# SBUF tensors allocated in another order: TensorE's split operands and the arena start at multiples of 1024 bytes

## The reference

```
for i in range(2):                                   # first block
    x = x + (attention if i == 0 else pooling)(rms_norm(x, norm_mix[i]))
    h = relu(rms_norm(x, norm_mlp[i]) @ w_up[i])     # 1024 x 4096
    x = x + (h * h) @ w_down[i]                      # 4096 x 1024
x = rms_norm(x, norm_final)
u = rms_norm(x) @ w_in                               # second block, 1024 x 7840
x = x + merge(gates, ssd(u) @ w_ssd_out, latent(u) @ w_mla_out) @ w_o
x = x + cross_attention(rms_norm(x), memory)         # w_xq, w_xkv, w_xo
y = sum over 2 of 32 experts: (silu(h @ w_gate[e]) * (h @ w_up[e])) @ w_down[e]
out = rms_norm(x + y)
```

## Time and profile before

| | before |
|---|---|
| median of 3 runs | 1366.15 us (1365.02 to 1366.16) |
| span of the profiled execution, first to last instruction | 1363.2 us |
| TensorE matmul busy | 1309.7 us, 9405 matmuls |
| VectorE busy | 1032.2 us |
| ScalarE busy | 872.8 us |
| DMA | 279.78 MB, mean 205 GB/s |
| mean granted TensorE clock | 0.992 |

### The profile page before, as it was taken

One profiled execution on the slowest core, in us unless ns is written; L12 is line 12 of the kernel. 1 busy time (PEld: TensorE's weight loads), 2 busy tenths in 40 slices (PEclk: granted clock), 3 DMA queues, 4 the chain that ended last, 5 costly groups with the idle time before them and its releaser, 6 DMA issues.

```text
span 1363.2 us, 23818 instructions
## 1 busy us (share of the span) xinstructions
PE 1309.7 (96%) x9405; PEld 1202.4 (88%) x9405; DVE 1032.2 (76%) x1535; ACT 872.8 (64%) x1289; POOL 78.2 (6%) x81
## 2 busy tenths in 40 slices
PE   7999999999999999999999899999998999999994
PEld 7989999998999998999999888999986777777773
DVE  6776655568555568998998886874569999999994
ACT  6565444546444546675656766654457999999994
POOL 0001000001000000000001100110000111011113
PEclk9999999999999999999999999999999999999997
DMA  8644555553655544555435534454436999999963
GB/s 276 205 152 130 191 185 185 185 186 94 202 185 187 187 140 145 178 161 158 150 102 181 193 122 155 155 186 161 157 156 254 365 360 354 351 366 365 362 261 123
DMA packets 150108, 279.78 MB, mean 205 GB/s; under 512 B 13721, under 2 KB 122238, under 8 KB 136574
## 3 DMA queue, kind: packets, MB, share of 16 engines
q1 hardware_dynamic: 141952, 269.97, 57.0%
q0 software_dynamic: 7696, 8.41, 2.0%
q10 hardware_dynamic: 366, 0.12, 0.0%
HBM read 274.26 MB, written 21.50 MB: 217 GB/s over the span
## 4 chain that ended last, share of the span: by engine, by line
PE 75%; DVE 15%; ACT 5%; issue 3%; DMA 1%; ACTq 0%; DVEq 0%; POOLq 0%; POOL 0%; SPq 0%
PE psum L852 18%; PE psum L854 18%; PE psum L853 18%; DVE weights_parts L2692 3%; PE psum L1413 3%; PE psum L1412 3%; PE psum L1411 3%; DVE weights_parts L2086 2%; PE psum L1437 2%; DVE arena L2476 2%; PE psum L1439 2%; PE psum L1438 2%; ACT weights_parts L1933 1%; ACT weights_parts L1476 1%; PE psum L1256 1%
## 5 line engine op out<-in xcount | busy, mean ns | idle before, releaser
L2086 DVE TENSOR_TENSOR weights_parts<-ring,weights_parts 128x1024 fp32r<-128x1024 f32 (+3 forms) x312 | 363.4, 1184 | 161.5 <-ACT weights_parts L1476 161.1
L1476 ACT ACTIVATE weights_parts<-ring 128x1024 fp32r<-128x1024 f32 (+3 forms) x312 | 309.0, 1010 | 175.6 <-PE psum L854 174.8
L852 PE MATMUL psum<-xnorm_parts,weights_parts 128*128 128x256 f32 x884 | 255.5, 289 | 6.0 <-DVE xnorm_parts L2235 2.0
L853 PE MATMUL psum<-xnorm_parts,weights_parts 128*128 128x256 f32 x884 | 249.0, 282 | 0.0
L854 PE MATMUL psum<-xnorm_parts,weights_parts 128*128 128x256 f32 x884 | 248.9, 282 | 0.0
L852 PE MATMUL psum<-expert_cols,weights_parts 128*128 128x256 f32 (+1 forms) x688 | 194.7, 283 | 3.3 <-DVE expert_cols L2104 2.0
L854 PE MATMUL psum<-expert_cols,weights_parts 128*128 128x256 f32 (+1 forms) x688 | 192.1, 279 | 0.0
L853 PE MATMUL psum<-expert_cols,weights_parts 128*128 128x256 f32 (+1 forms) x688 | 191.9, 279 | 0.0
L852 PE MATMUL psum<-hidden_parts,weights_parts 128*128 128x256 f32 x640 | 181.9, 284 | 2.6 <-DVE hidden_parts L2544 1.7
L853 PE MATMUL psum<-hidden_parts,weights_parts 128*128 128x256 f32 x640 | 180.5, 282 | 0.0
L854 PE MATMUL psum<-hidden_parts,weights_parts 128*128 128x256 f32 x640 | 180.5, 282 | 0.0
(11 more groups left out here) (422 smaller groups left out, 2528.3 us busy)
## 6 DMA issues: line engine op xcount, KB each, us to landing
expert_raw<-in_w_exp_down SPq DMA_DIRECT2D x35, 1024.0 KB, 7.6
ring<-in_mlp_w_up SPq DMA_DIRECT2D x32, 1024.0 KB, 5.4
ring<-in_mlp_w_down SPq DMA_DIRECT2D x32, 1024.0 KB, 4.9
ring<-in_w_in SPq DMA_DIRECT2D x30, 1024.0 KB, 5.3
ring<-in_w_exp_gate SPq DMA_DIRECT2D x23, 1024.0 KB, 5.0
ring<-in_w_exp_up SPq DMA_DIRECT2D x23, 1024.0 KB, 7.3
ring<-in_attn_w_qkv SPq DMA_DIRECT2D x12, 1024.0 KB, 8.4
expert_raw<-in_w_exp_gate SPq DMA_DIRECT2D x12, 1024.0 KB, 5.0
```

The lines of the kernel that those rows point to most:

```text
L852: pe.matmul(out, lh, rh, start=start, stop=False, **more)
L853: pe.matmul(out, lh, rl, start=False, stop=False, **more)
L1476: ins = act.activation(high, src, ACT.Copy)
L2086: ins = dve.tensor_tensor(low, src, high.bitcast(F32), ALU.subtract)
```

## The change

It reorders the calls of `sb`, and nothing else. Five small tensors come first (896 bytes together), then `weights_parts`, `xnorm_parts`, `hidden_parts`, the arena and its parts, then all the rest. No size, instruction or semaphore changes, and each engine has the same instructions in the same order (7240 rows on TensorE, 1100 on DVE, 958 on ACT, 28 on POOL, 246 on SP, all equal).

```diff
+        dtn = sb("dtn", [P, 5, SH])
+        dskip_all = sb("dskip_all", [P, SH])
+        dskip = sb("dskip", [P, ZT])
+        gain_both = sb("gain_both", [P, KT])
+        place_ids = sb("place_ids", [P, 8], I32)
+        w_parts = sb("weights_parts", [P, 2 * UNITS * UNIT], F32R)
+        x_parts = sb("xnorm_parts", [P, 2 * KT * TOK], F32R)
+        hid_parts = sb("hidden_parts", [P, 4 * 512], F32R)
+        with nc.sbuf_tensor("arena", [P, ARENA], F32) as arena:
+            pass
+        moe_units = sb("expert_parts", [P, M_RAW - M_UNITS], F32R)
+        moe_raw = sb("expert_raw", [P, M_COLS - M_RAW])
+        with nc.sbuf_tensor("expert_cols", [P, M_END - M_COLS], F32R) as moe_cols:
+            pass
+        results = sb("results", [P, M_END - M_COLS])
+        arena_rest = sb("arena_rest", [P, ARENA - M_END])
         ring = sb("ring", [P, SLOTS, SLOT])
         consts = sb("consts_sb", [P, C_N])
-        w_parts = sb("weights_parts", [P, 2 * UNITS * UNIT], F32R)
         cols = sb("cols", [P, 2 * P])
-        dskip = sb("dskip", [P, ZT])
-        dskip_all = sb("dskip_all", [P, SH])
...
-        x_parts = sb("xnorm_parts", [P, 2 * KT * TOK], F32R)
-        hid_parts = sb("hidden_parts", [P, 4 * 512], F32R)
...
-        with nc.sbuf_tensor("arena", [P, ARENA], F32) as arena:
-            pass
-        moe_units = sb("expert_parts", [P, M_RAW - M_UNITS], F32R)
...
-        arena_rest = sb("arena_rest", [P, ARENA - M_END])
         psum = ctx.enter_context(nc.psum_tensor("psum", [P, 8, 512], F32))
```

More of the change, by code:

```diff
@@ L364, in build_two_blocks @@
         std_col = sb("std_col", [P, 2, TB])
-        gain_both = sb("gain_both", [P, KT])
         smax = sb("smax", [P, 3, 2])
@@ L374, in build_two_blocks @@
         unit_pair = sb("unit_pair", [2 * SH, SH], F32R)
-        dtn = sb("dtn", [P, 5, SH])
         router_w = sb("router_w", [P, KT, EG + NE])
@@ L379, in build_two_blocks @@
         eps_col = sb("eps_col", [P, 3])
-        place_ids = sb("place_ids", [P, 8], I32)
         slot_rows = sb("slot_rows", [P, NB], I32)
```

## The result

| | before | after |
|---|---|---|
| median | 1366.16 us (4 runs, 1365.02 to 1366.27) | 1374.84 us (4 runs, 1374.51 to 1375.06) |
| ratio, with its 95% interval | 1 | 1.0065 (1.0051 to 1.0079) |
| span of the profiled execution | 1363.2 us | 1373.0 us |

The change costs 0.65%, 8.7 us. The forecast, 1348.0 us, had the wrong sign. The time lies inside the wide range of 1320 to 1386 us, in its slower part, because that range was stretched towards the slower rival. It lies outside the forecast's own 1335 to 1362 us. The rival that happened is "both streams in step", at a smaller price than it was given.

A forecast was written before the change was run, and what follows sets the result against it. TensorE, in flight 96% of the span, was taken as the bound, with DVE at 96% in the experts. 16.0 + 2.1 = 18.1 us off 1366.15 gave 1348.0 us; own range 1335 to 1362, 8 in 10: 1320 to 1386.

The forecast's parts named there:

- the wide range of 1320 to 1386 us: Whole kernel: range for 8 in 10, reaching to half of the much faster and half of the slower case.
- both streams in step: Every split matmul: equal left-overs make the reads collide, up to 122.5 and 245 ns, 1387 to 1408 us; chance 0.27.
- Matmuls of 256 columns: Split matmuls with tokens, expert_cols or weights moving: 21.8 us less TensorE time, of which 16.0 us reaches the end.
- Between them I take 115.0 ns: New distance of 256-column split matmuls, chosen between bounds of 107.5 and 122.5 ns.
- Two operands at the same left-over have shown 113.3: Reason given for 115.0 ns: weights moving, expert_cols stationary, both at 32 mod 64, ran at 113.3 ns.
- The shares passed on: Part of TensorE's 256-column gain reaching the end: 0.5 in 500 to 900 us (DVE at 85%), 0.9 elsewhere.
- Matmuls of 512 columns: Experts, 1260 matmuls: 233.3 to 230.0 ns, 4.2 us, half counted as DVE is at 96%: 2.1 us off.
- the straddled piece: Operand fetch in 64-byte pieces: 512-column moving weights 32 bytes off cover 33 pieces for 2048 bytes, fewer once aligned.
- DVE and ACT: Low parts take 1220 ns from ring and expert_raw alike, so no effect of place: cost 0.
- Transfers: Gate pieces land 5.0 us after issue; aligned destinations might save about 3% of a transfer, hidden by DVE: cost 0.
- The places don't matter: Rival for all streams: distances stay among the known ones, nothing happens, 1364 to 1368 us; chance 0.18.
- The count in 50 to 500 us: Quickest test in the profile after: TensorE matmuls in that stretch, 3693 before, about 3% more at 115.0 ns.

The follow-up runs named there:

- the half-low one of the change: Changed kernel with DVE writing only half of the low parts of the experts' weights from the 7th unit on: 1358.35 us, 0.9947.
- the second and fourth experiment: Changed kernel with 32 bytes ahead of xnorm_parts: 1360.48 us; changed kernel with weights_parts and xnorm_parts at 32, hidden_parts 64, arena 96: 1363.68 us.
- the half-low pair: Kernel before and changed kernel, each with DVE writing half of the experts' low weight parts from the 7th unit on: 1353.04 and 1358.35 us.
- the run at 80, 112 and 240: Changed kernel, weights 16 bytes later and padding, start differences 80 (xnorm_parts), 112 (hidden_parts), 240 (expert_cols): 1370.17 us, one run.

## Why the prediction was wrong, point by point

**The step that failed** is the one under "Matmuls of 256 columns": "Between them I take 115.0 ns". It was chosen from the left-over mod 64 of each operand by itself. What sets the distance of these tensors, all at multiples of 32, is the difference of the two starts mod 256. None of the pairs read in the earlier trace rows has the difference 0; they have 224, 64, 192 and 32. "Two operands at the same left-over have shown 113.3" took 32 and 32 mod 64 for the same place, but mod 256 that pair stands 192 apart. The rows could not give the number for 0, and the interpolation was read as if they could.

**The terms of the sum.** 118.3 to 120.0 ns costs 4572 x 1.7 = 7.8 us, 117.8 to 120.0 costs 2064 x 2.2 = 4.5, 116.7 to 120.0 costs 288 x 3.3 = 1.0. Another 192 matmuls, with the weights moving and expert_cols stationary, had no term in the prediction: 114.5 (three quarters at 113.3, one at 118) to 120.0, 1.1 us. Sum 14.4 us against the 21.8 off that was forecast. At the experts' start 12.3 of it have arrived, 0.85. The shares passed on had been put at 0.9, and at 0.5 in the stretch with DVE at 85%, and the half was about right. The weight loads that began at 500, 900 and 1000 us before begin 8.0, 10.5 and 12.3 us later. So 500 to 900 us adds 2.5 us, where the mean distances give 4.5 (2170 matmuls with xnorm_parts or hidden_parts moving, 400 with expert_cols, 48 with the weights), 0.56. The two other traces with these distances, the half-low one of the change and the old order with 32 bytes, show 2.5 us there as well. 50 to 500 us adds 8.0, 6.3 and 7.7 us in the three traces, where the distances give 6.9. So the share did not fail; the sign and the size of the distance did.

**Matmuls of 512 columns.** The sign was right, the size somewhat too small and the reason wrong: 226.7 ns with weights_parts moving against xnorm_parts, 229.2 with expert_parts moving and 229.8 in the down product, not 230.0, and the second and fourth experiment refute the straddled piece. 420 x 6.6 + 420 x 4.1 + 420 x 3.3 = 5.9 us of TensorE's time, of which 2.5 arrive, 0.4 and not quite "half". With DVE relieved, 5.5 arrive. That DVE caps it was right, and the half-low pair shows it.

**DVE and ACT** at no cost: right. The groups by form of the kernel after, which answer to the earlier trace rows:

```profile
L2692 DVE TENSOR_TENSOR expert_parts<-ring,expert_parts 128x1024 fp32r<-128x1024 f32 x46 | 55.2, 1218 | 0.0
...
L2692 DVE TENSOR_TENSOR expert_parts<-expert_raw,expert_parts 128x1024 fp32r<-128x1024 f32 x24 | 28.9, 1219 | 0.0
```

**Transfers** at no cost: right in the sum. By the Trainium skill, "DMA: Bandwidth & Descriptors", section "How a descriptor splits into AXI transactions", a row of 8192 bytes takes 32 transactions for 33 once its destination is aligned, as an estimate 3% less time. The landing times show no such gain, 5.4 and 5.2 us for 5.0, and the median packet of 8192 bytes takes 309 ns in both kernels. But the alignment does show in single packets, in the direction of the rule. Of the packets of 1024 bytes between 50 and 1000 us, 5.6 to 5.9% take longer than 46 ns, their median, in the three kernels whose ring starts at a multiple of 256 (the change, its half-low version, and the run at 80, 112 and 240), and 13.9 to 18.1% in the other eleven. That is worth little, mean 52.1 ns for 52.4, and no time here hangs on it.

**The rivals.** "The places don't matter" is out: 1.0065 against 1.0003 for the old left-overs in the new order. The Trainium skill, "TensorE: Matmul & The Clock Gate", part 2, with its two independent read ports, stood for that rival. Here the distance of the same instruction goes from 116.7 to 120.0 ns with the places of its two operands, so in this format the two reads are not independent in what they cost. "Both streams in step" has the right place (every split matmul of 256 columns) and the right condition (the same left-over). Its price, 122.5 ns, was taken from a strided stationary operand and was too high: 120.0. That strided stream takes 243 to 246 ns per 512 columns in all traces, at differences of 0, 32 and 64 alike, so it priced something else. In the experts it had the wrong sign, as there the same condition gives the fastest distance of all. With 120.0 and nothing for the experts it would have said 1366 + 14 = 1380.

**The bounds.** The forecast's own range doesn't quite follow from its terms: 28 us off is 1338 us and not 1335, and 117 ns everywhere gives about 6 us off, 1360 and not 1362. Neither changes the account.

**What the profile was to show.** All streams of 256 columns at one number: yes, but 120.0, above the 118.4 that was named as the sign of this rival. The count in 50 to 500 us fell by 1.9% instead of rising by 3%.

## What to carry to other kernels

Where TensorE is the bound and both operands are split fp32r data in SBUF, the byte where a tensor starts is a free parameter worth about 1%: look at the difference between the starts of moving and stationary operand mod 256, and read the distance between matmuls in the timeline. "Aligned to a large power of two" is no aim in itself; it puts all differences at 0, the slowest difference for 256 columns that tokens moving have shown, shared with 96. A few unused bytes between tensors are enough, and any edit that changes a tensor's size can shift the others by chance: the kernel before lost 0.7% by 32 bytes.

## What the runs showed of the hardware

Steady distance of split fp32r matmuls of 256 columns at the granted clock 1.00, over all kernels here, from pieces of at least 20 matmuls. Two values stand where pieces of one stream differ.

| d, both starts at multiples of 32 | ns |
|---|---|
| 0, 96 | 120.0 |
| 128 | 118.6 |
| 224 | 118.3 |
| 160 | 117.4 or 118.7 |
| 64, 192 | 117.8 or 113.3 |
| 32 | 116.7 (some pieces at 117.8, few at 120.0) |

In this table it makes no difference which of the two tensors moves, where both cases were measured (all but 96). It is otherwise where weights_parts starts 8 or 16 bytes off a multiple of 32. Most of these values come from a single run:

| d, weights_parts 8 or 16 off | tokens moving, ns | weights moving, ns |
|---|---|---|
| 16 | 117.3 or 120.0 | 116.7 or 118.6 |
| 80 | 118.1 | 119.5 |
| 176 | 118.7 | 119.2 |
| 240 | 118.4 | 117.2 |
| 24, 48 | 117.8, 116.7 | |
| 56 | 116.8 to 119.9 | |
| 88 | 113.3 or 120.0 | |
| 112 | 119.6 | |
| 168, 232 | | 120.0, 120.6 |
| 208 | | 119.0 or 117.0 |

So at such starts the difference alone no longer gives the distance, and a value for tokens moving can't be carried over to weights moving.

For 512 columns (means of a stream): 226.7 to 230.8 at d = 0, 229.4 and 229.9 at 64, 232.7 to 234.2 at 32, 96, 144, 160, 176, 192, 200, 208 and 224, 235.4 at 240 and 238.2 at 232. So the best difference for 256 columns is not the best for 512.

Three things stay open. The same addresses can settle at 113.3 or at 117.8 ns (d = 64 and 192, also in the earlier trace rows), so how the two reads meet at the start of a stream may count as well; no run here chose it. What changes within 32 bytes was not taken apart. And which part of the memory or of TensorE the reads share is not shown: the runs show the dependence on the difference, not its cause.
